# One decode step of a hybrid model: the samples' state products on row groups and 32-column strips of TensorE

## The reference

```python
# gated DeltaNet, 4 heads, S is 128 x 128: one token of a sample
u = beta * (v - exp(g) * (S^T k))
o = exp(g) * (S^T q) + (q . k) * u
S = exp(g) * S + k u^T
# gated linear attention (GLA), 4 heads, S is 64 x 128
S = diag(exp(log_a)) * S + k v^T
o = S^T (q * 64 ** -0.5)
```

## Time and profile before

| | |
|---|---|
| three runs, us | 2116.14, 2124.16 (median), 2126.21 |
| the profiled execution, us | 2123.61 |
| its span, us | 2121.8 |
| mean granted clock of TensorE | 0.959 |
| busy share: TensorE, VectorE, ACT, GpSimd | 94%, 24%, 18%, 6% |
| DMA, mean | 265 GB/s, 350 GB/s counting reads and writes at the memory |

### The profile page before, as it was taken

How to read it: one execution, slowest core, us unless ns; L and a number is a source line. 1 busy time by engine, 2 the same in 40 slices (tenths; PEclk the granted TensorE clock), 3 DMA queues, 4 the chain that set the end, 5 groups by cost and what they waited for, 6 DMA issues and landing times.

```text
span 2121.8 us, 28662 instructions
## 1 busy us (share of the span) xinstructions
PE 1996.3 (94%) x12236; PEld 1398.0 (66%) x12236; DVE 519.2 (24%) x1055; ACT 373.3 (18%) x762; POOL 121.9 (6%) x206
## 2 busy tenths in 40 slices
PE   8898889999989999999988899998969999999998
PEld 6787767878657888878877678876753333343333
DVE  3322244141722000033332432435340000000000
ACT  2221123233301000013111324341011100100001
POOL 2000000030410000000000001023000000000000
PEclk9999979899999999999998899999988999999999
DMA  9998547799979988567432466656363999949993
GB/s 306 343 363 282 184 168 261 256 334 311 390 280 346 378 305 313 214 238 266 149 125 99 149 207 222 245 191 237 120 219 134 371 358 405 393 147 386 370 409 143
DMA packets 254051, 563.06 MB, mean 265 GB/s; under 512 B 11629, under 2 KB 149073, under 8 KB 253648
## 3 DMA queue, kind: packets, MB, share of 16 engines
q1 hardware_dynamic: 235232, 500.14, 65.9%
q0 software_dynamic: 17904, 57.79, 8.3%
q10 hardware_dynamic: 784, 3.25, 0.4%
HBM read 547.34 MB, written 196.24 MB: 350 GB/s over the span
## 4 chain that ended last, share of the span: by engine, by line
PE 88%; DVE 3%; DMA 2%; ACT 2%; SPq 2%; issue 2%; DVEq 0%; ACTq 0%; POOL 0%; POOLq 0%
PE PS L762 34%; PE PS L1353 14%; PE PS L1379 7%; PE PS L867 4%; PE PS L1217 4%; PE PS L1257 4%; PE PS L755 3%; PE PS L1231 3%; PE PS L1315 2%; SPq L724 2%; PE PS L860 2%; PE PS L1401 1%; PE PS L1061 1%; PE PS L947 1%; PE PS L968 1%
## 5 line engine op out<-in xcount | busy, mean ns | idle before, releaser
L762 PE MATMUL PS<-h,ring 128*128 128x264 f32 x3328 | 792.9, 397 | 8.1 <-DMA ring<-in_w_in 6.4
L762 PEld LDWEIGHTS PS<-h,ring 128*128 128x128 f32 x3328 | 641.6, 196 | 142.1 <-issue 25.3
L1512 ACT COPY z<-PS 128x264 f32<-128x264 f32 (+3 forms) x307 | 131.1, 445 | 1024.7 <-PE PS L762 678.5
L1353 PE MATMUL PS<-ring,z 128*32 128x512 f32 (+1 forms) x1440 | 212.2, 527 | 1.2 <-ACT z L1512 1.2
L1353 PE MATMUL PS<-arena,z 128*32 128x512 f32 (+1 forms) x1056 | 190.1, 535 | 0.0
L1353 PEld LDWEIGHTS PS<-ring,z 128*32 128x32 f32 x1440 | 68.5, 111 | 126.9 <-issue 111.4
L1379 PE MATMUL PS<-arena,z 128*32 128x512 f32 x432 | 104.0, 593 | 0.0
L1353 PEld LDWEIGHTS PS<-arena,z 128*32 128x32 f32 x1056 | 55.0, 110 | 53.5 <-issue 53.4
L1217 PE MATMUL PS<-z,ring 128*128 128x264 f32 x384 | 87.3, 388 | 0.0
L1353 PE MATMUL PS<-z 128*32 128x512 f32 x576 | 84.7, 593 | 0.0
L1379 PE MATMUL PS<-ring,z 128*32 128x512 f32 x480 | 83.5, 592 | 0.0
(11 more groups left out here) (303 smaller groups left out, 1864.5 us busy)
## 6 DMA issues: line engine op xcount, KB each, us to landing
out_win_s<-in_cache_win_kv SPq DMA_DIRECT2D x128, 1023.5 KB, 10.0
ring<-in_w_in SPq DMA_DIRECT2D x88, 1024.0 KB, 5.7
out_win_s<-in_cache_win_kv SPq DMA_DIRECT2D x32, 1022.0 KB, 10.7
ring<-in_moe_w_gate SPq DMA_DIRECT2D x28, 1024.0 KB, 9.5
arena<-in_moe_w_up SPq DMA_DIRECT2D x22, 1024.0 KB, 11.7
ring<-in_moe_w_up SPq DMA_DIRECT2D x22, 1024.0 KB, 8.7
ring<-in_moe_w_down SPq DMA_DIRECT2D x20, 1024.0 KB, 11.0
arena<-in_moe_w_down SPq DMA_DIRECT2D x18, 1024.0 KB, 10.6
```

The lines of the kernel that those rows point to most:

```text
L762: last = mm(bank(*job)[:, 0:T], w(k), h[:, k, :], start=(k == 0), stop=(k == KT - 1))
L1353: last = mm(m_bank("c", "gu", g, b, w, r)[BLK * j:BLK * j + BLK, 0:n], hs[:, k, P * r + BLK * j:P * r + BLK * j + BLK], v3(slot_ap(set_slo ...
L1512: return nc.scalar.copy(out, in_)
```

## The change

It affects only the stage described above, once per layer.

- `gs_a`: VectorE scatters k and q into a zeroed buffer `wz` (4 x 256 columns; zeroed in `gdn_dec` 1), so that each pair of sample and head has a strip of 32 columns which is zero but for its two own. The strip is now stationary (128x32), the state moves (128 columns), head q takes column group q of the array, and the 8 samples accumulate in one bank. ACT copies the result, and a new step `gs_t` turns it over (`skt`); VectorE's work on u moves from `gs_b` to `gs_t`, the decay of the state with it.
- `gs_b`: u and k are turned over into all four groups of 32 partitions (8 matmuls), and one masked multiply of 128x1024 (constant `umask`) takes the place of four of 32x1024. `gs_c` is two steps of 4 matmuls, each matmul in another row group; the steps stand at other places of the list.
- GLA: keys and values turned over to all row groups, one masked multiply of 128x1024 (`gmask`), `gx_u` in one step on 4 row groups and 2 column groups, `gx_q` with q zero-padded in `qz_s` (stationary, 64x32) and the state moving, into one bank; a new step `gx_r` turns it over.
- The norm of `ob` becomes the last, n = 9.
- In the list, `gs_c` 0 stands after projection 44 instead of 42, and projections 51 to 54 stand otherwise around `gx_u` and `gx_q`; ahead of `kv_tok` stand the same 64 projections.

```diff
         for v in range(3):
             s += [("gdn_lv", i, v)] + p()
         s += [("gdn_st", i)] + p()
-    s += [("gs_a",)] + p() + [("gla_x",), ("gla_vb",)] + p() + [("gs_b",), ("gla_b",)] + p()
-    s += [("gla_g",), ("gla_e",)] + p() + [("norm_sq", 2), ("gs_c", 0)] + p() + [("norm_sum", 2), ("gs_c", 1), ("gla_k",)] + p()
-    s += [("gla_a", 0), ("gs_c", 2), ("norm_sq", 3)] + p() + [("gla_o", 0), ("gs_c", 3), ("gla_a", 1)] + p()
+    s += [("gs_a",)] + p() + [("gs_t",), ("gla_x",), ("gla_vb",)] + p() + [("gs_b",), ("gla_b",)] + p()
+    s += [("gla_g",), ("gla_e",)] + p() + [("norm_sq", 2)] + p(2) + [("norm_sum", 2), ("gs_c", 0), ("gla_k",)] + p()
+    s += [("gla_a", 0), ("gs_c", 1), ("norm_sq", 3)] + p() + [("gla_o", 0), ("gla_a", 1)] + p()
     s += [("gs_d",), ("norm_sum", 3), ("gla_o", 1), ("gla_ch", 0)] + p() + [("norm_sq", 4), ("gla_ch", 1)] + p()
     s += [("norm_sum", 4), ("gla_ch", 2)] + p() + [("norm_sq", 5), ("gla_ch", 3), ("gx_t",)] + p()
-    s += [("norm_sum", 5), ("gx_m", 0)] + p() + [("gx_u", 0), ("gx_m", 1)] + p() + [("gx_u", 1)] + p() + [("gx_q",)] + p()
-    for n in range(6, 10):
-        s += [("norm_sq", n)] + p() + [("norm_sum", n)] + p()
+    s += [("norm_sum", 5), ("gx_m",)] + p() + [("gx_u",)] + p(2) + [("gx_q",), ("norm_sq", 6)] + p() + [("gx_r",), ("norm_sum", 6)]
+    for n in range(7, 10):
+        s += p() + [("norm_sq", n)] + p() + [("norm_sum", n)]
+    s += p()
     s += p(64 - 21 - 18 - 16 - 8) + [("kv_tok",), ("att_sc", 0)]
     for t in range(AH // 2):
...
+    n8 = np.arange(8)[None]
+    put("umask", (row % 32 == 16 * (n8 // 4) + 4 * (row // 32) + n8 % 4) * 1.0)
+    put("gmask", (row % 32 - 24 == 4 * (row // 32 % 2) + np.arange(4)[None]) * 1.0)
...
-              + [(ob, 0, "ones", 1.0 / BDV, par[:, R_BO:R_BO + 1])]
-              + [(z, Z_K + 4 * n, "blk", 1.0 / DH, par[:, R_KN:R_KN + 1]) for n in range(3)])
+              + [(z, Z_K + 4 * n, "blk", 1.0 / DH, par[:, R_KN:R_KN + 1]) for n in range(3)]
+              + [(ob, 0, "ones", 1.0 / BDV, par[:, R_BO:R_BO + 1])])
...
             def gs_a(l):
                 pe.wait_ge(s0_in, 16 * (l + 1))
                 open_bank(pe, l, "skq")
+                pe.wait_ge(sems["wz_ready"], V("wz_ready", l))
                 for b in range(NS):
                     for q in range(CH):
-                        n = CH * b + q
-                        last = mm(bank(l, "skq")[:, 2 * n:2 * n + 2], S0[:, n, :], c[:, q:q + 5:4, NP_TOK + b],
-                                  start=True, stop=True)
+                        last = mm(bank(l, "skq")[32 * q:32 * q + 32, 0:P], wz[:, 256 * q + 32 * b:256 * q + 32 * b + 32],
+                                  S0[:, CH * b + q, :], start=(b == 0), stop=(b == NS - 1))
...
+            def gs_t(l):
+                wait_read(pe, l, "skq")
+                open_bank(pe, l, "skt")
+                turn_over(bank(l, "skt")[:, 0:P], kqs, P).then_inc(full(l, "skt"), 1)
+
             def gs_b(l):
                 open_bank(pe, l, "suk")
                 pe.wait_ge(sems["gs_o"], V("gs_o", l))
-                turn_over(bank(l, "suk")[0:32, 0:P], s_u, P)
-                turn_over(bank(l, "suk")[0:32, P:2 * P], s_k, P).then_inc(full(l, "suk"), 1)
+                for w, v_ in enumerate((s_u, s_k)):
+                    for r in range(4):
+                        last = mm(bank(l, "suk")[32 * r:32 * r + 32, P * w:P * w + P], v_, ident, start=True, stop=True)
+                last.then_inc(full(l, "suk"), 1)
 
             def gs_c(l, m):
                 wait_read(pe, l, "suk")
-                pe.wait_ge(sems["um_ready"], V("um_ready", l, m))
-                for n in (2 * m, 2 * m + 1):
-                    open_bank(pe, l, "su", n)
-                    mm(bank(l, "su", n), uk_sb[:, P:2 * P], um[m % 2][:, 4 * (n % 2):4 * (n % 2) + 4, :],
-                       start=True, stop=True).then_inc(full(l, "su", n), 1)
+                pe.wait_ge(sems["um_ready"], V("um_ready", l))
+                for r in range(4):
+                    rows = slice(32 * r, 32 * r + 32)
+                    open_bank(pe, l, "su", 4 * m + r)
+                    mm(bank(l, "su", 4 * m + r), uk_sb[rows, P:2 * P], um[rows, 4 * m:4 * m + 4, :],
+                       start=True, stop=True).then_inc(full(l, "su", 4 * m + r), 1)
 
             def gla_x(l):
...
-            def gx_u(l, t):
+            def gx_u(l):
                 wait_read(pe, l, "gk")
-                for n in (2 * t, 2 * t + 1):
+                pe.wait_ge(sems["vm_ready"], V("vm_ready", l))
+                for n in range(4):
                     open_bank(pe, l, "gu", n)
-                    for w in range(2):
-                        q = 2 * t + w
-                        pe.wait_ge(sems["vm_ready"], V("vm_ready", l, q))
-                        last = mm(bank(l, "gu", n)[64 * w:64 * w + 64, :], g_k[:, 64 * q:64 * q + 64],
-                                  vm[w][:, 4 * (n % 2):4 * (n % 2) + 4, :], start=True, stop=True)
-                    last.then_inc(full(l, "gu", n), 1)
+                for w in range(2):
+                    for n in range(4):
+                        rows = slice(32 * n, 32 * n + 32)
+                        last = mm(bank(l, "gu", n)[64 * w:64 * w + 64, :], g_k[rows, 64 * w:64 * w + 64], vm[rows, w],
+                                  start=True, stop=True)
+                        if w:
+                            last.then_inc(full(l, "gu", n), 1)
 
             def gx_q(l):
                 for n in range(4):
                     wait_read(pe, l, "gu", n)
-                for w in range(2):
-                    open_bank(pe, l, "gq", w)
-                    half = slice(64 * w, 64 * w + 64)
-                    for t in range(2):
-                        for b in range(NS):
-                            last = mm(bank(l, "gq", w)[:, 8 * t + b:8 * t + b + 1], g_s0[half, t, b, :],
-                                      z[half, Z_BQ + t, NP_TOK + b:NP_TOK + b + 1], start=True, stop=True)
-                    last.then_inc(full(l, "gq", w), 1)
+                pe.wait_ge(sems["qz_ready"], V("qz_ready", l))
+                open_bank(pe, l, "gq")
+                for b in range(NS):
+                    for j in range(BH):
+                        t, half = j // 2, slice(64 * (j % 2), 64 * (j % 2) + 64)
+                        last = mm(bank(l, "gq")[32 * j:32 * j + 32, 0:P], qz_s[half, t, 32 * b:32 * b + 32],
+                                  g_s0[half, t, b, :], start=(b == 0), stop=(b == NS - 1))
+                last.then_inc(full(l, "gq"), 1)
+
+            def gx_r(l):
+                wait_read(pe, l, "gq")
+                open_bank(pe, l, "gr")
+                turn_over(bank(l, "gr")[:, 0:P], gqs, P).then_inc(full(l, "gr"), 1)
 
             def kv_tok(l):
...
-                elif n == 6:
+                elif n == 9:
                     wait_read(act, l, "gi", 3)
-                    wait_read(act, l, "gq", 1)
+                    wait_read(act, l, "gr")
...
+                copy(uk_sb, bank(l, "suk")[:, 0:256]).then_inc(free(l, "suk"), 1)
 
             def gla_g(l):
...
                 return t_.rearrange("p (b h) -> p b h", b=NS)
 
             def gs_a(l):
+                for w in range(2):
+                    last = cp(v3(wz, 4)[:, :, w:w + 239:34], c[:, 4 * w:4 * w + 4, NP_TOK:T])
+                last.then_inc(sems["wz_ready"], 1)
...
                 wait_full(dve, l, "sgb")
                 link(cp(s_bc, bank(l, "sgb")[:, 0:64].rearrange("p (n b h) -> p n b h", n=2, b=NS)))
                 dve.drain().then_inc(free(l, "sgb"), 1)
-                wait_full(dve, l, "skq")
-                kq = bank(l, "skq")[:, 0:64].rearrange("p (b h w) -> p b h w", b=NS, h=CH)
+                wait_full(dve, l, "skt")
+                kq = bank(l, "skt")[:, 0:P].rearrange("p (h x) -> p h x", h=CH)[:, :, 0:2 * NS].rearrange(
+                    "p h (b w) -> p b h w", w=2)
                 link(tt(v4(s_u), kq[:, :, :, 1], s_bc[:, 0], MUL))
                 link(tt(v4(s_u), by_bh(c[:, 8:12, NP_TOK:T]), v4(s_u), SUB))
...
+            def gs_b(l):
                 wait_read(dve, l, "suk")
-                outer(l, 0)
-
-            def outer(l, n):
-                tt(um[n % 2], bc(uk_sb[:, 0:P], 1, [32, 8, P]), bc(ident[0:32, 8 * n:8 * n + 8], 2, [32, 8, P]),
-                   MUL).then_inc(sems["um_ready"], 1)
+                tt(um, bc(uk_sb[:, 0:P], 1, [P, 8, P]), bc(K("umask"), 2, [P, 8, P]), MUL).then_inc(sems["um_ready"], 1)
...
             def gs_c(l, n):
-                if n:
...
-            def add_outer(l, n):
                 dve.wait_ge(sems["s_state"], V("s_state", l))
-                for m in (2 * n, 2 * n + 1):
+                for m in range(4 * n, 4 * n + 4):
                     wait_full(dve, l, "su", m)
                     tt(S0[:, 4 * m:4 * m + 4, :], S0[:, 4 * m:4 * m + 4, :], v3(bank(l, "su", m), 4), ADD).then_inc(
                         free(l, "su", m), 1)
+
+            def gs_d(l):
```

(53 more changed lines are left out.)

57 lines of the change are left out of this document (20 added, 37 removed).

## The result

The changed kernel takes 2030.53 us (median of 4 runs, 2029.31 to 2032.72), the one before 2124.09 (4 runs). The ratio is 0.956, interval 0.954 to 0.959. On a second chip it was 2033.81 against 2125.64, 0.957 (0.955 to 0.959). The forecast was 2043, with a range of 2030 to 2064.

What follows compares the result with a forecast made beforehand. TensorE was taken to bound the kernel (88% of the chain). Work, waits and clock gave -42.6 us per layer, -85.2 for two; +3.6 clock and +1.4 tables made -80.2, from 2123.6 to 2043.4, range 2030 to 2064.

Steps and rivals of the forecast that it cites:

- the low clock behind the new wait: Before `gx_u`: a wait of 1.65 us would be followed by half clock in both layers, +1.8 us each.
- TensorE's own work: Changed stage: shorter `gs_a`, `gs_c`, `gx_u` and `gx_q`, less some added small matmuls, -27.8 us per layer.
- The added small rows: Two turn-overs and 6 more matmuls each in `suk` and `gx_t` on TensorE, +0.5 us per layer.
- B: Tile blocks: each record costs a least time whatever its columns, +3.8 us per layer, total 2051; chance 0.14.
- C: `gs_c`, `gx_u`: row groups don't work at once, 2060, chance 0.08; milder, row halves can't share a bank, 2047, 0.07.
- Waits: TensorE's holes in the stage: 2.42 and 5.42 us nearly go, smaller new waits come, -5.5 us per layer.
- Clock: Stage work that ran at 0.50 and is not removed, 18.5 us, would run at 1.00: -9.3 us per layer.
- A: Stage: the clock falls again around new tile blocks or waits, two more stretches per layer, 2064; chance 0.10.
- E: Whole stage: low clock holds over the shorter, denser stage, up to 2228, slower than before; chance 0.03.
- Once: Bias tables in layer 0: the norm of `ob` as norm 9 has a second VectorE operation, +1.4 us.
- Rival D: Layer 0 attention stage: DMA backlog delays cache loads, +5 to +12 us, 2048 to 2055; chance 0.05.

Runs made afterwards that it cites:

- serial_cols: Changed kernel with the two loops of `gs_a` and of `gx_q` exchanged, so eight matmuls in a row use one column group: 2047.89 us.
- one_row_group: Changed kernel with all matmuls of `gs_c` and `gx_u` reading rows 0 to 31 instead of four row groups (results wrong, timing only): 2062.67 us.
- later_steps: Changed kernel with the second `gs_c` and `gx_u` each one projection later and the norm of `ob` as number 7 instead of 9: 2029.00 us.
- narrow_a: Changed kernel with only the `gs_a` read products back in their old form, 2 columns moved and no turn-over: 2055.35 us.
- narrow_q: Changed kernel with only the `gx_q` read products back in their old form, one column moved and no turn-over: 2057.26 us.
- hole: Changed kernel with seven more chained VectorE memsets ahead of the GLA mask multiply, so TensorE waits longer before `gx_u`: 2049.89 us.
- before_again: The kernel before the change, unaltered, run for a second profile: 2121.26 us (one run).
- narrow_both: Changed kernel with both read products, `gs_a` and `gx_q`, back in their old narrow form: 2074.69 us.

## Why the prediction was right

The mechanism came as forecast in its three parts, work, waits and clock: the stage shows -43.0 us per layer and the forecast had -40.8. One step failed, the low clock behind the new wait, and two small terms were mis-sized.

- **TensorE's own work** was forecast at -27.8 per layer. `gs_a` and `gx_q` are 1.88 net, not 1.7, `gs_c` 1.07 and `gx_u` 1.05, not 0.92: 0.6 us per layer too low in the four blocks. The added small rows are 0.8, not 0.5. That makes -26.9. That the tiles work side by side, by columns and by row groups, is shown by `serial_cols` and `one_row_group`. Rivals B and C are out: 64 records in 1.88 us are 0.029 each, and `gx_q`, whose upper and lower row halves write one bank (each its own 32 partitions of it), takes no longer than `gs_a`, which has no halves. The Trainium skill, page "TensorEngine Tiling (Array Packing)", section "Restrictions and Gotchas", says that different row tiles can't use one PSUM bank at the same time; the trace does not agree for this block, where no cost of it can be seen. The 62 ns per matmul that the Trainium skill's page "TensorE: Matmul & The Clock Gate", section "Wait — 56ns, not 53.3ns?", gives for hardware decode off did not apply, as the 0.029 us per record shows.
- **Waits** were forecast at -5.5 per layer. Both large holes went entirely (-7.84, not -7.6); the pause in `gs_c` 1 is 1.06 (forecast 1.5), the hole before `gx_u` 1.42, +0.4 (forecast +0.6; by the prediction's own rows it should have been +0.5): -6.4. That the two new ones are waits for VectorE's adds and masks, `later_steps` shows: a projection more ahead of them removes both. Which of the edits removed the two large holes (the earlier chain, the single mask multiply, the other places in the list) no run took apart.
- **Clock**, forecast at -9.3 per layer: there is no low clock left in the stage, as forecast, and both reasons given hold by themselves: narrow products (`narrow_a`, `narrow_q`) and holes (`hole`) each lower it. Rivals A and E are out. The step that failed is the one that took 1.8 us back in each layer for a wait of 1.65 before `gx_u`: the clock stayed at 1.00 behind 1.42 us of wait in both layers. The mistake is +3.6 in all. The step was read off one stretch, in layer 1 of one profile; layer 0 of that profile and both layers of `before_again` have none behind the same wait. One case in four was taken for a rule. Why the clock fell that once is open.
- **Once**, forecast at +1.4 for the tables. In the first profiles VectorE's wait rose from 1.71 to 2.10, +0.4. In the second ones it rose from 1.26, and that a wait for TensorE, to 2.43, +1.2. So the term lies between these, and no run could isolate it.
- **Rival D**: the first wait for the cache loads in layer 0 grew from 5.67 to 6.53 us. Summed over both layers TensorE waited 11.7 us for them before, and 12.0 in the changed kernel: nothing like the 5 to 12 us of the rival.

The three parts together are -42.6 of the -43.0 per layer; the last 0.4 isn't assigned. Of the 13 us between the forecast of 2043 and the measured time, 4.3 are in the stage (3.6 of them the clock behind the wait), up to 1 is the tables', and the rest, 7 to 8 us, lies outside, where I had assumed that two executions are alike. So the stage is no luck, but the last step to the whole time is: the scatter outside, 12 us over the twelve profiles, is larger than the 7 to 8 us that fell away there, and had one microsecond more fallen away, the time would have been under 2030.

The change is worth, by parts and per layer: the two read products 19.6 us (`narrow_both`), of which 8.0 us only because four column groups work at once (`serial_cols`), and 23.3 us all the rest, of which 15.0 hang on the row groups (`one_row_group`), 6.8 of these by the clock. The 8.3 us left over are about as much as the two large holes (7.84).

## What to carry to other kernels

Small products on TensorE can cost more than their row: each of the two narrow blocks here (1 and 2 columns moved) brought 10 to 14 us of half clock with it, about half of it on the dense work behind. Pad them to tiles which lie side by side, move the long operand, and order the loop so that neighbours use different tiles; the same matmuls in the other order took three times as long. Then look again for the waits: what was hidden under a slow block is now in the open, and here one projection more ahead of it was enough. And before a stretch of low clock goes into a forecast, see whether a second profile of the same kernel has it at the same place.
